# Fetching the experts' rows and adding their outputs by indirect transfers in a two-layer mixture-of-experts trunk

## What is computed

```python
def _rmsnorm(x, g):
    xf = x.astype(jnp.float32)
    y = xf * lax.rsqrt(jnp.mean(xf * xf, axis=-1, keepdims=True) + EPS)
    return (y * g.astype(jnp.float32)).astype(x.dtype)

def _moe(h, router, w_gate, w_up, w_down):
    xf = h.reshape(T, D)                                # T = 256 tokens, D = 1024
    logits = (xf @ router).astype(jnp.float32)          # 8 experts
    top_logits, top_idx = lax.top_k(logits, 2)
    gates = jax.nn.softmax(top_logits, axis=-1)
    ...
    def expert_block(args):
        xb, e = args
        return (jax.nn.silu(xb @ w_gate[e]) * (xb @ w_up[e])) @ w_down[e]   # 1024 x 3584, 3584 x 1024
    ...
    out = jnp.zeros((T, D), h.dtype).at[buf_tok].add((yg * buf_gate[:, None]).astype(h.dtype))

def reference(x, ...):
    h = x
    h = h + _mixer_mla_retention(_rmsnorm(h, ab_norm[0]), ...)
    h = h + _swiglu(_rmsnorm(h, ffn_norm[0]), ...)
    h = h + _mixer_swa_stickbreak(_rmsnorm(h, cd_norm[0]), ...)
    h = h + _moe(_rmsnorm(h, moe_norm[0]), moe_router[0], moe_w_gate[0], moe_w_up[0], moe_w_down[0])
    return _rmsnorm(h, final_norm)
```

## Time and profile before

| what | value |
|---|---|
| median of 3 runs | 1661.13 us (1658.96 to 1662.04) |
| the profiled execution's own time | 1661.01 us |
| its span, first to last instruction | 1659.2 us |
| PE busy | 1598.3 us, 96% |
| DVE busy | 1262.7 us, 76% |
| ACT busy | 1089.9 us, 66% |
| POOL busy | 0.2 us |
| DMA, mean over the span | 268 GB/s |
| granted TensorE clock, mean | 0.978 |

### The profile page before, as it was taken

The page is one execution under the profiler, slowest core; times in us unless marked ns, Lnnn a source line. Parts: engine busy times, 40 slices in busy tenths (PEclk is TensorE's granted clock), DMA queues, the critical chain, the costliest instruction groups (busy, mean ns, idle before and its releaser), DMA issues.

```text
span 1659.2 us, 23233 instructions
## 1 busy us (share of the span) xinstructions
PE 1598.3 (96%) x7968; PEld 1335.7 (81%) x7968; DVE 1262.7 (76%) x1454; ACT 1089.9 (66%) x1320; POOL 0.2 (0%) x4
## 2 busy tenths in 40 slices
PE   7988989999999898999999999999999999999995
PEld 6867889999977677888888888888888888888884
DVE  4446555444566547999999999999999999999995
ACT  5434454444455545877877877877877877877874
POOL 0000000000000000000000000000000000000000
PEclk9997899999999998999999999999999999999998
DMA  9630355556543336999998998999998999998950
GB/s 328 193 140 1 103 192 188 178 186 217 179 153 127 115 121 256 369 368 334 365 376 320 365 376 320 360 371 329 359 381 321 361 368 333 369 371 320 372 202 27
DMA packets 190325, 444.36 MB, mean 268 GB/s; under 512 B 7872, under 2 KB 17984, under 8 KB 190016
## 3 DMA queue, kind: packets, MB, share of 16 engines
q1 hardware_dynamic: 190272, 443.68, 74.5%
HBM read 442.61 MB, written 1.05 MB: 267 GB/s over the span
## 4 chain that ended last, share of the span: by engine, by line
PE 94%; DVE 3%; ACT 2%; issue 1%; DMA 0%; DVEq 0%; ACTq 0%; SPq 0%
PE bank L259 28%; PE bank L261 28%; PE bank L260 28%; PE bank L1544 2%; PE bank L1715 1%; PE bank L1216 1%; PE bank L814 0%; PE bank L1209 0%; PE bank L1737 0%; PE bank L821 0%; PE bank L1738 0%; PE bank L412 0%; PE bank L1202 0%; PE bank L1201 0%; PE bank L1231 0%
## 5 line engine op out<-in xcount | busy, mean ns | idle before, releaser
L272 DVE TENSOR_TENSOR w_lo<-ring,w_hi 128x1024 fp32r<-128x1024 f32 (+1 forms) x834 | 1003.5, 1220 | 263.3 <-ACT w_hi L268 224.3
L268 ACT ACTIVATE w_hi<-ring 128x1024 fp32r<-128x1024 f32 (+1 forms) x834 | 879.7, 1059 | 370.4 <-PE bank L261 369.4
L259 PE MATMUL bank<-w_hi,xe_hi 128*128 128x512 f32 x896 | 354.4, 396 | 1.4 <-DVE xe_lo L1536 1.4
L261 PE MATMUL bank<-w_hi,xe_lo 128*128 128x512 f32 x896 | 350.3, 391 | 0.0
L260 PE MATMUL bank<-w_lo,xe_hi 128*128 128x512 f32 x896 | 349.2, 390 | 0.0
L259 PEld LDWEIGHTS bank<-w_hi,xe_hi 128*128 128x128 f32 x896 | 168.3, 188 | 37.3 <-DVE w_lo L272 1.9
L261 PEld LDWEIGHTS bank<-w_hi,xe_lo 128*128 128x128 f32 x896 | 168.1, 188 | 36.2
L260 PEld LDWEIGHTS bank<-w_lo,xe_hi 128*128 128x128 f32 x896 | 168.5, 188 | 34.2
L259 PE MATMUL bank<-w_hi,hT_hi 128*128 128x512 f32 x448 | 177.9, 397 | 1.4 <-DVE hT_lo L1632 1.4
L261 PE MATMUL bank<-w_hi,hT_lo 128*128 128x512 f32 x448 | 176.9, 395 | 0.0
L260 PE MATMUL bank<-w_lo,hT_hi 128*128 128x512 f32 x448 | 176.8, 395 | 0.0
(11 more groups left out here) (259 smaller groups left out, 1583.3 us busy)
## 6 DMA issues: line engine op xcount, KB each, us to landing
ring<-m_gate_dram SPq DMA_DIRECT2D x112, 1024.0 KB, 6.4
ring<-m_up_dram SPq DMA_DIRECT2D x112, 1024.0 KB, 6.4
ring<-m_down_dram SPq DMA_DIRECT2D x112, 1024.0 KB, 6.1
ring<-ab_w_in_dram SPq DMA_DIRECT2D x16, 936.0 KB, 6.0
ring<-f_gate_dram SPq DMA_DIRECT2D x14, 1024.0 KB, 5.0
ring<-f_up_dram SPq DMA_DIRECT2D x14, 1024.0 KB, 5.0
ring<-f_down_dram SPq DMA_DIRECT2D x14, 1024.0 KB, 4.9
ring<-cd_w_in_dram SPq DMA_DIRECT2D x11, 1024.0 KB, 4.9
```

The lines of the kernel that those rows point to most:

```text
L259: nc.tensor.matmul(out_, a_hi, b_hi, start=first, stop=False, **kw)
L261: return nc.tensor.matmul(out_, a_lo, b_hi, start=False, stop=last, **kw)
L268: nc.scalar.activation(w_hi[:, buf, 0:width], src, ACT.Copy).then_inc(hi_ready, 1)
L272: nc.vector.tensor_tensor(w_lo[:, buf, 0:width], src, f32(w_hi[:, buf, 0:width]), ALU.subtract).then_inc(split_ready, 1)
```

## The change

Two tables go to memory: `h_rows`, the residual with 128 spare rows behind it, and `xn_rows`, the normed rows. POOL writes both at the start of the stage.

- *Row numbers.* `rows_pe`: two products of `pick` with `tok_gate` (token number + 1, and the gates of the eight experts, 9 columns) give for each place its token and its gate. `rows_dve` turns that into `row_from` (what to fetch), `row_next` (where to add; places without a token go to spare rows) and `gate_next`. For expert q+1, PE does this in chunk 2 of expert q and DVE in chunk 3.
- *Gather.* For experts 1 to 7 of the loop POOL fetches 128 rows of `xn_rows` by `row_from` to `xe_rows`, and PE turns them (`turn_rows`, eight transposes) in place of the 16 products. Expert 0 still uses the products.
- *Scatter.* For experts 0 to 6 ACT writes the scaled output in float32 to `y_rows`, and POOL adds it to `h_rows` by `row_to` in memory. Then it raises `row_free`, for which DVE waits in chunk 2 of the next expert before it overwrites `place_gate` and `row_to`. Expert 7 keeps the products; ahead of its adds POOL brings `h` back from `h_rows`.
- *Turned intermediate.* `hT_hi` and `hT_lo` have two buffers. At the end of an expert, turn(6) stands between the halves of down(5), and ACT and DVE do hT of chunk 6 after two units of d(6), not three.

```diff
-        hT_hi = place("hT_hi", [P, 4, CAP], F32R, at=ARENA + 4096)
-        hT_lo = place("hT_lo", [P, 4, CAP], F32R, at=ARENA + 6144)
+        hT_hi = [place(f"hT_hi{i}", [P, 4, CAP], F32R, at=(ARENA + 4096, XT_AT + 4096)[i]) for i in range(2)]
+        hT_lo = [place(f"hT_lo{i}", [P, 4, CAP], F32R, at=(ARENA + 6144, XT_AT + 6144)[i]) for i in range(2)]
...
+        def turn_rows(pe, r):
+            for kk in range(4):
+                k = 4 * r + kk
+                ins = nc.tensor.transpose(pb[2 + r][:, kk * P:kk * P + P], xe_rows[:, k * P:k * P + P],
+                                          const("ident"))
+            ins.then_inc(gather_banked, 1)
...
-        def prepare_gates(dve, e, part):
...
+        def rows_pe(pe, q):
+            pe.wait_ge(pick_done, 2 * q + 2)
             for tb in range(TB):
+                ins = nc.tensor.matmul(pb[7][:, 0:NE + 1], pick[:, tb, :], tok_gate[:, tb, :], start=tb == 0,
+                                       stop=tb == 1)
+            ins.then_inc(rows_banked, 1)
+        def rows_dve(dve, e, q, part):
+            dve.wait_ge(rows_banked, q + 1)
+            found = pb[7][:, 0:1]
+            nc.vector.tensor_scalar(spare_row, found, 0.0, const("spare"), ALU.is_equal, ALU.mult).then_inc(spare_done, 1)
+            nc.vector.tensor_scalar(row_from, found, -1.0, 0.0, ALU.add, ALU.max)
+            nc.vector.tensor_copy(gate_next, pb[7][:, one(e + 1)])
+            dve.wait_ge(spare_done, q + 1)
+            nc.vector.scalar_tensor_tensor(out=row_next, in0=found, scalar=-1.0, in1=spare_row, op0=ALU.add,
+                                           op1=ALU.add).then_inc(rows_done, 1)
+        def moe_gp(gp, part):
+            q0 = NE * part
+            if part:
+                gp.wait_ge(sc_done, 4 * part + 4)
+            else:
+                gp.wait_ge(h_done, 4 * 3)
+            gp.dma_start(h_rows[0:256, :].rearrange("(b p) d -> p b d", p=P), h).then_inc(h_out, 16)
+            if not part:
+                gp.wait_ge(rows_scaled, TB)
+                gp.dma_start(xn_rows.rearrange("(b p) d -> p b d", p=P), xn).then_inc(xn_out, 16)
+            for q in range(q0, q0 + NE - 1):
+                gp.wait_ge(rows_done, q + 2)
+                gp.wait_ge(gather_banked, 2 * q + 2)
+                gp.wait_ge(xn_out, 16)
+                gp.indirect_dma_start(out=xe_rows, out_offset=None, in_=xn_rows,
+                                      in_offset=bass.IndirectOffsetOnAxis(ap=row_from, axis=0)).then_inc(rows_in, 16)
+                gp.wait_ge(row_ready, q + 1)
+                gp.wait_ge(y_scaled, 2 * q + 4)
+                gp.wait_ge(h_out, 16 * (part + 1))
+                gp.indirect_dma_start(out=h_rows, out_offset=bass.IndirectOffsetOnAxis(ap=row_to, axis=0),
+                                      in_=y_rows, in_offset=None, compute_op=ALU.add).then_inc(added, 16)
+                gp.wait_ge(added, 16 * (q - part + 1))
+                gp.sem_inc(row_free, 1)
+            gp.dma_start(h, h_rows[0:256, :].rearrange("(b p) d -> p b d", p=P)).then_inc(h_back, 16)
+            gp.wait_ge(h_back, 16 * (part + 1))
...
-                nc.scalar.activation(hT_hi.rearrange("p j t -> p (j t)"), pb[6], ACT.Copy).then_inc(hT_done, 1)
-            def outputs(q):
+                if c >= 2:
+                    act.wait_ge(*m_used("d", c - 2, q))
+                else:
+                    act.wait_ge(unit_used, UPE * q + (U_MOE + NBUF))
+                nc.scalar.activation(hT_hi[c % 2].rearrange("p j t -> p (j t)"), pb[6], ACT.Copy).then_inc(hT_done, 1)
...
+                act.wait_ge(row_ready, q + 1)
                 for n in range(2):
-                    nc.scalar.activation(y_hi[:, n * 512:n * 512 + 512], pb[4 + n], ACT.Copy,
-                                         scale=place_gate).then_inc(y_hi_done, 1)
+                    dst = y_hi if last else y_rows
+                    nc.scalar.activation(dst[:, n * 512:n * 512 + 512], pb[4 + n], ACT.Copy,
+                                         scale=place_gate).then_inc(y_scaled, 1)
...
-                m_hi(act, ("d", LAST), q, slice(0, 3))
+                m_hi(act, ("d", LAST), q, slice(0, 2))
                 turned(LAST, q)
-                m_hi(act, ("d", LAST), q, slice(3, 4))
+                m_hi(act, ("d", LAST), q, slice(2, 4))
...
-            def add(q):
+            def add():
+                dve.wait_ge(h_back, 16 * (part + 1))
...
+                    if c == 2:
+                        dve.wait_ge(row_free, q + (1 - part))
+                        nc.vector.tensor_copy(place_gate, gate_next)
+                        nc.vector.tensor_copy(row_to, row_next).then_inc(row_ready, 1)
+                    if c == 3 and not last:
+                        dve.wait_ge(row_ready, q + 1)
+                        rows_dve(dve, e + 1, q + 1, part)
                 m_lo(dve, ("d", LAST - 1), q, slice(0, 3))
                 product(LAST, q)
                 m_lo(dve, ("d", LAST - 1), q, slice(3, 4))
-                m_lo(dve, ("d", LAST), q, slice(0, 3))
+                m_lo(dve, ("d", LAST), q, slice(0, 2))
                 rest(LAST, q)
-                m_lo(dve, ("d", LAST), q, slice(3, 4))
-                if not last:
-                    for r in range(2):
-                        gather_dve(dve, r, q + 1)
-                    m_lo(dve, ("g", 0), q + 1, slice(0, 3))
-                outputs_rest(q)
-                if not last:
-                    m_lo(dve, ("g", 0), q + 1, slice(3, 4))
-                    m_lo(dve, ("u", 0), q + 1)
-                add(q)
+                m_lo(dve, ("d", LAST), q, slice(2, 4))
+                if last:
+                    outputs_rest(q)
+                    add()
+                    return
+                for r in range(2):
+                    gather_dve(dve, r, q + 1)
+                m_lo(dve, ("g", 0), q + 1)
+                m_lo(dve, ("u", 0), q + 1)
...
-            prepare_gates(dve, 0, part)
             m_lo(dve, ("u", 0), q0)
+            rows_dve(dve, 0, q0, part)
...
+                    if c == 2 and not last:
+                        pe.wait_ge(rows_done, q + 1)
+                        rows_pe(pe, q + 1)
                     gate_up("u", c, q)
-                    down(c - 1, q)
+                    if c < LAST:
+                        down(c - 1, q)
+                down(LAST - 1, q, slice(0, 2))
                 turn(LAST, q)
+                down(LAST - 1, q, slice(2, 4))
                 if last:
                     down(LAST, q)
-                    scatter(q)
+                    scatter()
                     return
-                pe.wait_ge(pick_done, 2 * q + 4)
+                pe.wait_ge(rows_in, 16 * (q + (1 - part)))
                 for r in range(2):
-                    gather_pe(pe, r)
+                    turn_rows(pe, r)
                 down(LAST, q)
                 first(q + 1)
-                scatter(q)
...
             gate_up("u", 0, q0)
+            pe.wait_ge(gates_done, 1)
+            rows_pe(pe, q0)
```

More of the change, by code:

```diff
@@ L8 @@
 I32 = mybir.dt.int32
+U32 = mybir.dt.uint32
 ALU = mybir.AluOpType
@@ L220, in trunk @@
                              "moe_done"))
[L221 to L226, removed]
+        pick_done, y_scaled, pickT_done = (sem(n) for n in ("pick_done", "y_scaled", "pickT_done"))
+        rows_banked, spare_done, rows_done, row_ready, gates_done = (
+            sem(n) for n in ("rows_banked", "spare_done", "rows_done", "row_ready", "gates_done"))
+        h_out, xn_out, rows_in, added, row_free, h_back = (
+            sem(n) for n in ("h_out", "xn_out", "rows_in", "added", "row_free", "h_back"))
+        gather_banked, gather_hi, gathered, pgt_banked, e_silu, e_prod, h_banked, hT_done, hT_lo_done, y_done, \
+            sc_banked, sc_done = (
+                sem("e_" + n) for n in ("gather_banked", "gather_hi", "gathered", "pgt_banked", "silu", "prod",
+                                        "h_banked", "hT", "hT_lo", "y", "sc_banked", "sc_done"))
         posm = rt[:, 0:16].rearrange("p (e t) -> p e t", t=TB)
-        gate = rt[:, 16:32].rearrange("p (e t) -> p e t", t=TB)
-        place_gate = rt[:, 440:441]
         class Steps:
@@ L1660, in expert @@
                     if c == 1:
-                        dve.wait_ge(pgt_done, q + 1)
-                        nc.vector.tensor_scalar(pickT.rearrange("p b t -> p (b t)"), pb[7][:, 0:256], 0.0, None,
-                                                ALU.is_gt).then_inc(pickT_done, 1)
-                    if c == 1 and not last:
-                        prepare_pick(dve, e + 1, part)
-                        prepare_gates(dve, e + 1, part)
+                        if last:
+                            dve.wait_ge(pgt_banked, part + 1)
+                            nc.vector.tensor_scalar(pickT.rearrange("p b t -> p (b t)"), pb[7][:, 0:256], 0.0, None,
+                                                    ALU.is_gt).then_inc(pickT_done, 1)
+                        else:
```

(16 more changed lines are left out.)

73 lines of the change are left out of this document (39 added, 34 removed).

## The result

The changed kernel takes **1630.88 us** (median of 4 runs, 1629.90 to 1631.02) beside 1660.05 for the kernel before (4 runs, 1658.96 to 1662.04): ratio 0.9818, interval 0.9806 to 0.9831. Forecast was 1632.5. Its profiled execution took 1629.9 us, span 1628.0, against 1661.0 and 1659.2, so the two traces differ by 31.2 us.

The account below looks back on a forecast made before the run. PE's instruction stream was taken to bound the kernel; terms -17.3 - 12.9 - 2.0 + 3.5 - 1.65 + 1.8 summed to -28.5 us, taking 1661.0 to 1632.5 us. Range 1625 to 1652.

Parts of the forecast that it names:

- The bound: Expert stage: PE's stream sets the pace, one expert taking 124.5 us, as long as DVE and the DMA engines hold.
- Gather: PE, seven of eight experts: 8 transposes (1.10 us) replace 16 fp32 products (3.57 us), 17.3 us gained.
- Scatter: PE, all experts but the last: eight matmuls of 1.84 us in all go, 12.9 us gained.
- gate transposes: PE, all experts but the last: two transposes of 0.14 us each go, 2.0 us gained.
- Row numbers: PE, all eight experts: two added fp32 matmuls of 9 columns, 0.44 us an expert, 3.5 us lost.
- Tail: Last expert: PE's 1.65 us wait for hT_lo before down(6) goes with two buffers and the earlier turn, 1.65 us gained.
- The second buffer: Seven other experts: avoids an hT_lo wait the shorter gather would uncover, worth up to 3.9 us otherwise given back.
- Start of expert 0: Before g(1), DVE's reading of row numbers delays PE 2.2 us once, 0.44 already counted: 1.8 us lost.
- Rival 1: The accumulate outlasts its 41 us of room before DVE's copy, delaying weight splits; 1695.5 us at X = 50; 8%.
- 7 x (X - 41): Loss over seven experts if y to row_free takes X us; the gain is eaten at X = 45.
- Rival 2: GpSimd's 14 indirect issues and DVE's w_lo splits hinder each other; a 2.5 us stop gives 15 us, 1648; 15%.
- Rival 3: DMA engines become the bound in the expert stage: at 354 GB/s 27 us lost, 1660 us; 7%.

Follow-up runs that it names:

- Run 5: Changed kernel with all experts gathered by products again, memory accumulate and two hT buffers kept: 1648.08 us, ratio 0.9924.
- run 6: Kernel before with only two buffers of hT and the moved last turn added: 1656.92 us, ratio 0.9976.
- run 4: Changed kernel with one buffer of hT again and the last turn back behind all of down(5): 1640.45 us, ratio 0.9872.
- run 7: Changed kernel with four more fetches of 128 rows, each waited for, between accumulate and row_free: 1630.01 us, ratio 0.9813.
- run 8: Changed kernel with seven more fetches of 128 rows, each waited for, between accumulate and row_free: 1754.09 us, ratio 1.0566.
- run 10: Changed kernel with expert 0's row numbers early, arena 128 bytes further, and y_lo handed over by halves in the last scatter: 1614.47 us, ratio 0.9723.
- run 11: Changed kernel with the arena moved 64 bytes further, to 192 modulo 256: 1624.52 us, ratio 0.9783.
- run 12: Changed kernel with the arena moved 256 bytes further, still 128 modulo 256: 1630.66 us, ratio 0.9813.
- run 1: Changed kernel with PE making expert 0's row numbers ahead of up(0) instead of behind it: 1626.13 us, ratio 0.9783.
- run 2: Changed kernel with the places of the even and odd chunks' hT exchanged: 1628.28 us, ratio 0.9796.
- run 3: Changed kernel with the whole arena moved 128 bytes further, to a multiple of 256: 1616.45 us, ratio 0.9739.
- run 9: Changed kernel with expert 0's row numbers early and the arena 128 bytes further, together: 1615.57 us, ratio 0.9727.

## Why the prediction was right

- *The bound.* PE's stream set the time before and after, as read from the earlier trace rows; no engine and no transfer took its place.
- *Gather.* 2.47 us an expert foreseen, 2.58 measured; a transpose of fetched rows cost 0.124 us, the turn's 0.14. Run 5's medians give 17.2 us for the term of 17.3, but its periods say 19.0 (its gather took 3.68 and not 3.57): the term is right within 2 us, the match to 0.1 is chance.
- *Scatter* and *gate transposes*: 1.84 as said; 0.22 for 0.28. Runs 5 and 6 bear them out together.
- *Row numbers*: 0.45 us for 0.44. *Tail*: the wait of 1.65 became 0.29 and not nothing, 1.4 gained; but the half clock in the last scatter gave 1.2 of it back.
- *The second buffer* was called worth up to 3.9 us that would otherwise be lost in the middle experts; run 4 shows 5.4. What the prediction didn't see is the place: half of the downs moved from an offset of 128 to one of 0, 3 x 0.14 us an expert. This is the larger part of what the period gained beyond the forecast (4.91 instead of 4.15 us an expert, 4.6 us over six periods); the rest is the small w_lo wait and the gather.
- *Start of expert 0.* The wait was right (2.2 us), the half clock behind it, 1.5 us, was not in the sum.
- *The sum*, -28.5, stands against -29.2 by the medians and -31.2 by the two traces. The time, 1632.5, is right within 2 us, the gain within 3, and part of that is luck: two terms that the sum lacked go against each other, the place of hT, about 4 us gained, and the half clock, 1.5 and 1.2 lost.
- *Rival 1* fell by the landing of 6.3 us against 41 of room; runs 7 and 8 show that the room is as large as was read from the earlier trace rows and that what lies beyond it costs: 17.9 us an expert for 16.7 us beyond it, the rest being mostly the half clock, which the rule 7 x (X - 41) left out.
- *Rival 2* fell by one row, w_lo's durations, minimum, median and maximum, beside those that the kernel before had from 700 to 1600 us (1214/1225/1228 as well):

```profile
L283 DVE TENSOR_TENSOR w_lo<-ring,w_hi x633: 1214/1225/1228, 699.5 to 1598.7; 128x1024 fp32r<-128x1024 f32 x159
```

  and not even beside a fetch's issue is one longer; five splits take 6.10 us here:

```profile
829.81 6.10 DVE L283 TENSOR_TENSOR w_lo<-ring,w_hi 128x1024 fp32r<-128x1024 f32 x5
```
```profile
830.15 1.75 POOL L1612 DMA_INDIRECT xe_rows<-xn_rows,row_from  x1 [56.28 <-DVE row_next L1593]
```

  By the Trainium skill, "SBUF — State Buffer", on the shared port pair, the two should contend when GpSimd reads SBUF. These rows show no such loss while it writes descriptors; an instruction of GpSimd that reads tiles ran in no kernel here.
- *Rival 3* fell too: landings of loads are 5.6 to 6.2 us by line (6.1 to 6.4 before), ACT waits for PE and not for the ring, slices reach 404 GB/s, and run 7 moved more without loss. The limit of some 358 GB/s that "DMA: Bandwidth & Descriptors" of the Trainium skill gives for a core under "Specifications" did not hold as one here, where one core ran alone.

## What to carry to other kernels

Where one engine's stream is the chain and an operation on it only moves rows, give it to a queue and count two things: the instructions that leave the stream, and the room until somebody needs what the queue frees. Here 31 us of TensorE's time (7 x 2.58 and 7 x 1.84) became 23 us of an idle GpSimd, with 6 us of landing in 41 us of room; up to that edge delay was free (run 7), and beyond it each microsecond cost one or a little more (run 8). When work that covered a wait is removed, look at what it covered: the second buffer as such was worth 1 us with the long gather and 6 with the short one. And try the start address of tiles that TensorE holds stationary: moving one arena by 128 bytes was worth half as much as the whole change (14.4 us by the medians, 1.1 of it by the clock in the last scatter).

## What the hardware did that was not expected

- Matmuls of 512 columns whose stationary operand starts at 128 modulo 256 bytes took 232.5 ns from start to start (5.58 us for 24); at 0 they took 226.7 (5.44) and at 192 229 (5.49). Over the kernel: 14.4 us of 1631, of which 2.7 ahead of the experts and 5 in them are traced to such groups.
- Some two microseconds of idle TensorE can be followed by the 1.2 GHz level for about 3 us, as after 2.22 us at the start of expert 0. In the last scatter the wait was 2.64 to 2.66 us in every kernel but run 10's. The lower level followed for nearly all its products in the changed kernel and in runs 8, 11 and 12 (2.7 to 2.9 us for seven of them instead of 1.57), for a part in runs 1, 6 and 7, and not at all in the kernel before nor in runs 2, 3, 4, 5 and 9. So the wait's length alone doesn't decide it; what does stays open.
- An indirect transfer of 128 rows of 4 KB landed 6.0 us (fetch) or 6.3 us (accumulate) after its issue, medians of seven each among loads that fill the queues, as quickly as a plain load of 1 MB (5.6 to 6.2), and held GpSimd 1.75 and 1.58 us.
